# One phase of a two-block transformer kernel: the squares, sums and norm of the memory tokens in other slots of the output projection

## What is computed

```python
h = h + hybrid_mixer(rms_norm(h, norm_mix_g), ...)          # ends with concat([o, c]) @ w_out
h = h + memory_cross_attention(rms_norm(h, norm_xa_g),
                               rms_norm(mem, norm_mem_g), xa_wq, xa_wk, xa_wv, xa_wo)

# in the mixer, o comes from a gated delta rule with 8 heads of 128, c from a convolution:
o = rms_norm(o, dn_norm_g) * silu(z)       # the output norm, a mean of squares over each head
c = silu(layer_norm(c, cf_ln_g, cf_ln_b))
return concat([o, c], axis=-1) @ w_out     # phase "wout"

# rms_norm(x, g) = x * rsqrt(mean(x * x, axis=-1) + 1e-6) * g
k = mem_n @ w_k                            # phase "memk", the next one
```

## Time and profile before

| | us |
|---|---|
| median of 3 runs | 2903.57 |
| lowest, highest | 2901.63, 2904.53 |
| the profiled execution, its time | 2901.38 |
| its span, first to last instruction | 2899.6 |
| TensorE busy | 2817.0 |
| VectorE busy | 2066.1 |
| ScalarE busy | 1357.9 |

### The profile page before, as it was taken

One profiled execution on the slowest core, in us unless ns is written; L12 is line 12 of the kernel. 1 busy time (PEld: TensorE's weight loads), 2 busy tenths in 40 slices (PEclk: granted clock), 3 DMA queues, 4 the chain that ended last, 5 costly groups with the idle time before them and its releaser, 6 DMA issues.

```text
span 2899.6 us, 55174 instructions
## 1 busy us (share of the span) xinstructions
PE 2817.0 (97%) x23814; PEld 2768.6 (95%) x23814; DVE 2066.1 (71%) x2866; ACT 1357.9 (47%) x1723; POOL 4.6 (0%) x12
## 2 busy tenths in 40 slices
PE   7999998999999999999999999999989999999998
PEld 7999998999999999999999999997789999999998
DVE  7988755888869787787777866545566665675675
ACT  4445453444434553544545545455445544553453
POOL 0000000000000000000000000000000000000000
PEclk9999998999999999999999999999999999999999
DMA  6555204678747777777777765433245566556553
GB/s 237 182 175 165 68 8 155 209 275 288 261 152 250 288 279 279 285 282 283 293 275 273 277 219 189 163 122 124 89 149 199 194 198 191 194 188 201 191 188 124
DMA packets 160516, 591.59 MB, mean 204 GB/s; under 512 B 17840, under 2 KB 17840, under 8 KB 159760
## 3 DMA queue, kind: packets, MB, share of 16 engines
q1 hardware_dynamic: 159408, 580.45, 57.9%
q0 software_dynamic: 864, 7.60, 0.7%
HBM read 585.88 MB, written 2.10 MB: 203 GB/s over the span
## 4 chain that ended last, share of the span: by engine, by line
PE 88%; DVE 7%; ACT 2%; issue 1%; DMA 1%; SPq 0%; DVEq 0%; ACTq 0%
PE bank L485 79%; DVE wlo L1597 2%; PE bank L827 1%; DVE modacc L1583 1%; PE bank L690 1%; PE bank L505 1%; ACT whi L1015 1%; PE bank L704 1%; PE bank L522 1%; PE bank L526 1%; PE bank L795 1%; PE bank L805 1%; DVE tmp L1776 0%; PE bank L794 0%; PE bank L514 0%
## 5 line engine op out<-in xcount | busy, mean ns | idle before, releaser
L485 PE MATMUL bank<-act,whi 128*128 128x256 f32 x10144 | 1765.2, 280 | 44.3 <-DVE wlo L1597 28.7
L485 PEld LDWEIGHTS bank<-act,whi 128*128 128x128 f32 x10144 | 1546.3, 190 | 50.2 <-DVE wlo L1597 25.8
L1597 DVE TENSOR_TENSOR wlo<-raw,whi 128x1024 fp32r<-128x1024 f32 x906 | 1096.5, 1222 | 453.0 <-ACT whi L1015 450.9
L485 PE MATMUL bank<-act,wlo 128*128 128x256 f32 x5072 | 1413.9, 279 | 0.0
L1015 ACT ACTIVATE whi<-raw 128x1024 fp32r<-128x1024 f32 x906 | 943.3, 1057 | 779.2 <-PE bank L485 778.5
L485 PEld LDWEIGHTS bank<-act,wlo 128*128 128x128 f32 x5072 | 962.5, 190 | 0.0
L485 PE MATMUL bank<-hid,whi 128*128 128x256 f32 x3456 | 590.2, 277 | 1.5 <-DVE wlo L1597 1.5
L485 PEld LDWEIGHTS bank<-hid,whi 128*128 128x128 f32 x3456 | 520.8, 188 | 1.9 <-DVE wlo L1597 1.3
L485 PE MATMUL bank<-hid,wlo 128*128 128x256 f32 x1728 | 478.2, 277 | 0.0
L1583 DVE SCALAR_TENSOR_TENSOR modacc<-modraw,small,modacc 128x512 f32<-128x512 f32 x480 | 348.3, 746 | 18.9 <-DMA modraw<-mods 13.6
L485 PEld LDWEIGHTS bank<-hid,wlo 128*128 128x128 f32 x1728 | 324.9, 188 | 0.0
(11 more groups left out here) (363 smaller groups left out, 1519.5 us busy)
## 6 DMA issues: line engine op xcount, KB each, us to landing
raw<-stream SPq DMA_DIRECT2D x906, 512.0 KB, 4.6
modraw<-mods SPq DMA_DIRECT2D x192, 512.0 KB, 4.5
h<-x_t SPq DMA_DIRECT2D x4, 512.0 KB, 5.2
memV<-mem_t POOLq DMA_DIRECT2D x1, 2048.0 KB, 8.5
tmp<-ctx_t POOLq DMA_DIRECT2D x1, 2048.0 KB, 9.7
out_t<-tmp SPq DMA_DIRECT2D x4, 512.0 KB, 2.6
cz<-catt POOLq DMA_DIRECT2D x1, 1216.0 KB, 11.6
bias<-na_bias POOLq DMA_DIRECT2D x1, 1024.0 KB, 5.2
```

The costliest lines, as they stand in the source:

```text
L485: mm = pe.matmul(b[:, hf * T:(hf + 1) * T], lhs, rhs, start=(kc == 0 and hf == 0 and n == 0), stop=(kc == ph.chunks - 1 and n == 2), skip_ ...
L1597: ve.tensor_tensor(wlo[:, at % SPL_N, :], raw[:, at % RAW_N, :], whi[:, at % SPL_N, :].bitcast(F32), ALU.subtract).then_inc(split_done, 1)
```

## The change

Three things are moved or exchanged:

- ScalarE's four squares of memory go from (0, 4), all at once, to (1, 0) to (1, 3), one per slot, with the wait for the load at (1, 0).
- VectorE's four strided reductions at (0, 7) become, one quarter per slot at (1, 1) to (1, 4), two plain additions each: 128x512, then 128x256.
- The steps of the norm follow: row sums from (1, 3) to (1, 7), mean from (1, 6) to (2, 2), square root from (1, 7) to (2, 3), reciprocal from (2, 0) to (2, 4), spreading from (2, 2) to (2, 5).
- On TensorE, slot 1 comes ahead of the row sums of the output norm, directly behind slot 0.

```diff
             def memory_root(i, j):
-                if (i, j) == (1, 3):
+                if (i, j) == (1, 7):
                     pe.wait_ge(mem_sum, 1)
...
-                if (i, j) == (2, 2):
+                if (i, j) == (2, 5):
                     norm_root(3, ROOT, root)
...
-            c.at(act_ready, 1)
-            next(wout)
+            for n in range(2):
+                c.at(act_ready, n + 1)
+                next(wout)
             for hd in range(DN_H):
                 c.at(on_act, hd // 4 + 1)
                 for mt in range(TT):
                     mm = row_sums(bank[4][:, 2 * hd + mt:2 * hd + mt + 1], tmp[:, hd, :], slice(mt * P, (mt + 1) * P), True, True)
             mm.then_inc(on_pe, 1)
-            c.at(act_ready, 2)
-            next(wout)
             c.at(on_dve, 2)
...
             def memory_squares(i, j):
-                if (i, j) == (1, 7):
+                if (i, j) == (2, 3):
                     c.at(var, 1)
                     sc.activation(small[:, ROOT:ROOT + TT], small[:, ROOT:ROOT + TT], ACT.Sqrt).then_inc(std, 1)
                     c.end(var, 1)
-                if isinstance(i, int) and i == 0 and j == LAG + 1:
-                    sc.wait_ge(mem_in, 16)
-                    for q in range(4):
-                        sc.activation(tmp[:, 4 * q:4 * q + 4, :], memory[:, 4 * q:4 * q + 4, :], ACT.Square).then_inc(mem_sq, 1)
+                if i == 1 and j < 4:
+                    if j == 0:
+                        sc.wait_ge(mem_in, 16)
+                    sc.activation(tmp[:, 4 * j:4 * j + 4, :], memory[:, 4 * j:4 * j + 4, :], ACT.Square).then_inc(mem_sq, 1)
...
             def memory_sums(i, j):
-                if (i, j) == (1, 6):
+                if (i, j) == (2, 2):
                     c.at(sums, 1)
...
-                if (i, j) == (2, 0):
+                if (i, j) == (2, 4):
                     c.at(std, 1)
...
-                if isinstance(i, int) and i == 0 and j == PH["wout"].S - 1:
-                    for q in range(4):
-                        c.at(mem_sq, q + 1)
-                        ins = ve.tensor_reduce(memK[:, q, :],
-                                               tmp[:, 4 * q:4 * q + 4, :].rearrange("p k t -> p t k"), AX.X, ALU.add)
-                    ins.then_inc(mem_sum, 1)
+                if i == 1 and 1 <= j <= 4:
+                    q = j - 1
+                    c.at(mem_sq, q + 1)
+                    sq = tmp[:, 4 * q:4 * q + 4, :]
+                    chain(ve.tensor_tensor(sq[:, 0:2, :], sq[:, 0:2, :], sq[:, 2:4, :], ALU.add))
+                    ins = ve.tensor_tensor(memK[:, q, :], sq[:, 0, :], sq[:, 1, :], ALU.add)
+                    if q == 3:
+                        ins.then_inc(mem_sum, 1)
```

## The result

The changed kernel takes 2888.58 us (median of 4 runs, 2887.83 to 2889.97). The kernel before took 2904.05 us beside it (4 runs, 2901.63 to 2905.33). The ratio is 0.9945, with an interval of 0.9934 to 0.9957: faster by 12.5 to 19.2 us, the medians 15.5 apart. The forecast was 2890.8, in a range of 2887.5 to 2896.0. The profiled execution took 2889.14 us, its span is 2887.3; the profiled pair is thus 12.2 us apart in time and 12.3 in span. Among the experiments' executions, one of experiment 1 (4750.46 us) and one of the kernel before beside it (3165.69 us) had a granted clock of 0.56 and 0.84 where all others have 0.99; the medians count them, the ratios do not.

The account below looks back on a forecast made before the run. TensorE, busy 97% of the span, was taken as the bound, so only its stalls or lower clock pay. 12.8 + 0.4 - 0.4 = 12.8 us off 2901.38 gave 2888.6; 2.2 for the median made 2890.8, range 2887.5 to 2896.

Parts of the forecast that it names:

- (a): TensorE slots 5 to 7: waits of 7.67 and 2.34 us go, slot 8 starts at 467.6 instead of 480.41, 12.8 us won.
- (b): Second body: the moved squares and additions fit on ScalarE and VectorE beside TensorE's 22.6 us; cost taken as zero.
- (c): ScalarE's moved wait for memory, behind the split of slot 8: under a microsecond of waiting, counted as zero cost.
- late-memory rival: Memory lands beyond 465.5 us as raw loads take half of the bytes, costing 1 to 4 us; chance 0.08.
- (d): Memory's norm, moved later: VectorE's waits for row sums and spread cost TensorE zero, one microsecond if VectorE's idle time is gone.
- (e): Output norm at the phase's start, slot 1 ahead of the row sums: gain between -0.1 and 0.85 us, 0.4 taken.
- (f): TensorE's full-clock pace, 113.5 or 118 ns per multiplication: slots 8 to 11 may keep the slower one; -0.4 us taken.
- Slower: Rival: pace falls to 118 ns in long stretches behind the phase; 600 us of it gives 2914.8 us; chance 0.03.
- Does the gain stay: Behind the phase: the next phase's 3.5 us entry stall stays and comes earlier by the same time, gain expected whole.

Follow-up runs that it names:

- experiment 1: Changed kernel with TensorE's old order put back (slot 0, output norm's row sums, slot 1): 2890.29 us, ratio 0.9953 to the kernel before.
- experiment 9: The changed kernel itself run once more, nothing edited, beside three variants: 2889.02 us, ratio 0.9945 to the kernel before.
- Experiment 5: Changed kernel with the four squares and their wait for memory's load back at (0, 4) on ScalarE: 2901.33 us, ratio 0.9990 to the kernel before.
- experiment 4: Kernel before with eight additions replacing the four strided reductions at the old place (0, 7): 2902.53 us, ratio 0.9995 to the kernel before.
- experiment 3: Changed kernel with strided reductions, one per slot at the new places, instead of the two additions: 2892.55 us, ratio 0.9961 to the kernel before.
- experiment 6: Changed kernel with POOL's two transfers swapped, so memory comes behind the 1.2 MB one: 2891.46 us, ratio 0.9953 to the kernel before.
- experiment 2: Kernel before with only slot 1 put ahead of the output norm's row sums on TensorE: 2906.99 us, ratio 1.0007 to the kernel before.
- Experiment 8: Changed kernel with TensorE's spreading of memory's root one slot later, at (2, 6): 2890.23 us, ratio 0.9949 to the kernel before.

## Why the prediction was right, point by point

**(a) The two stalls: right.** 12.8 us were forecast for the start of slot 8; from slot 3 to slot 8, 12.73 came, and 13.24 in the second profile of the changed kernel (experiment 9). Slot 5 starts directly behind slot 4, at 457.57. Experiment 5 shows which edit does it (12.3 us of it back with the squares in the first body), experiment 4 how little the reductions were (2.1).

**(b) The second body has room: right.** The additions take 0.68 and 0.43 us as in the earlier trace rows; TensorE doesn't wait there. That even reductions of 2.05 us would have fitted (experiment 3) the sum didn't ask.

**(c) The moved wait: the size was off, the price wasn't.** "Under a microsecond" was 2.42. Two terms made it: ScalarE was done with the split of slot 8 at 459.0 and not 460.4, as TensorE ran about 1.6 us earlier from slot 3 on; and memory landed at 461.4 and not 460.8. It cost nothing, since a lead of 3.0 us was left behind it (experiment 6). The load lands so late because it is issued late, at 452.3 us before and 452.1 after, when TensorE is in slot 2 or 3: the memset that it waits for is ahead of the phase in VectorE's order only. Whether it could be issued earlier was not tried.

The late-memory rival is out, and its premise, weight loads that take half of the bytes, did not come. The queues (packets, MB, share) while memory was under way, first in the changed kernel with five weight loads beside it, then before with one, answer to the earlier trace rows:

```profile
q0 software_dynamic: 191, 2.55, 74.0%
q1 hardware_dynamic: 107, 0.44, 11.4%
...
raw<-stream SPq DMA_DIRECT2D x5, 512.0 KB, 10.4
memV<-mem_t POOLq DMA_DIRECT2D x1, 2048.0 KB, 9.3
```

```profile
q0 software_dynamic: 172, 2.37, 72.1%
q1 hardware_dynamic: 87, 0.36, 10.2%
```

Five loads moved hardly more than one. Memory needed 9.3 us here and 8.5 before, but 9.2 to 9.5 in experiments 2, 4 and 5 too, which have one load beside it, and 8.9 to 9.8 in the others with POOL's transfers in this order. So the 0.8 us is not the loads' doing; the 8.5 us is the lowest of the thirteen. The rival's sum took 2.85 MB for what POOL's queue moved up to the landing, where the trace has 2.37: with that, its own halving lands memory near 463.6, short of both 464.3 and 465.5.

The Trainium skill (DMA: Bandwidth & Descriptors, Queues, rings and completion order) has each engine take turns between the rows it has work for, a whole packet at a time. By that and the packet sizes of these lines (13.4 KB against 4.1), an estimate, memory's queue would keep some 77%, if the packets of the profile are those of the page. This trace has 85% up to the landing, and 74% over 452.1 to 465 us (3.34 of 4.50 MB, the landed memory and then the 1.2 MB behind it), so the rule is not borne out here by its numbers; that it gave the landing at 461.6, with 2.85 MB in the sum, was luck.

**(d) Memory's norm: right.** VectorE waits 2.13 us for the sums (2.02 before) and 0.79 for the spread, TensorE for neither. Experiment 8 shows that 3.50 would be free as well. The changed kernel's VectorE timeline:

```profile
490.78 0.16 DVE L1997 TENSOR_SCALAR small<-bank 128x2 f32<-128x2 f32 x1 [2.13 <-PE bank L522]
```

**(e) The output norm: right in size, by terms at the edges of what was given.** TensorE's timeline, and the stretch in which the spreading starts, answer to the earlier trace rows:

```profile
436.78 3.63 PE L522 MATMUL bank<-ones,tmp 128*128 128x1 f32 x32
...
441.20 5.47 PE L526 MATMUL bank<-ident,small 128*128 128x128 f32 x32 [0.80 <-DVE small L1980]
449.04 0.50 PE L485 MATMUL bank<-act,whi 128*128 128x256 f32 x2 [2.37 <-DVE act L1989]
...
441.00:444.00 3.00, 2.80 (x13) 2.80 (x14) 0.90 (x2) 0.00 (x0) 0.00 (x0) 0.55 0.00 0
```

The spreading starts 9.96 us behind slot 0 instead of 10.82, 0.86 us won where 0.85 was said. It falls to half clock, as feared, and takes 5.47 us instead of 3.73, so that slot 2 comes 0.4 us later behind slot 0 than before. In return slot 2 runs at full clock, 2.84 us instead of 4.24. Net, 1.0 us by slot 3 where 0.4 were taken, inside the stated -1.5 to 2.2. All of it is the order's own (experiment 1 takes 21.65 us to slot 3, as before), and without the memory part it is nothing in the total (experiment 2). Its two parts, the earlier spreading and the clock in slot 2, were both named; the 0.4 was the middle of a range and no sum.

**(f) Pace: the mechanism right, the size too small.** 0.4 us were charged (the three figures given there add up to 0.3), and from slot 8 to the next phase the changed kernel lost 1.5 (70.35 us against 68.86). It holds 118 ns over the last ten slots of the phase, where before has 113.5. The same kernel profiled again (experiment 9) doesn't. Both for 516 to 524 us, L485 alone, with the columns of the earlier trace rows:

```profile
516.00:524.00 8.00, 8.00 (x70) 8.00 (x69) 1.00 0.72 260
```

```profile
516.00:524.00 8.00, 8.00 (x73) 8.00 (x72) 1.00 0.76 268
```

Experiment 9's phase is 103.0 us long, the first profile's 105.2, both of one kernel. So this term is not fixed by the kernel, and should have been a spread of some 2 us and not -0.4. Whether the change makes the slower pace more frequent is open: the last eight slots of the phase take 22.6 us in five of the fourteen profiles, all of kernels with both parts of the change (nine profiles), and 21.8 us in the other four of these and in all five without. The rival "Slower" asked for 600 us at the slower pace; behind slot 4 of the next phase the ledger moves by 0.6 us in all, over 2300 us.

**Does the gain stay: yes, within about a microsecond.** The entry stall of the next phase went from 3.5 to 3.1 us (3.5 in experiment 9):

```profile
PE bank L485 <- DVE wlo L1596: 3.1, 1, 3.1
```

From there the gain stays at 12.3 us up to the context load, loses 0.8 there, comes back by 1.3 near 2150 us, where nothing was edited, and is 12.8 at the last slot.

**The total.** For the profiled execution 2888.6 us were forecast and 2889.14 came. The mechanism carries this, but the closeness is in part luck. In the ledger the forecast's 12.8 + 0.4 - 0.4 came as 12.73 + 1.02 - 1.48, and 0.60 us won ahead of the phase, for which the sum had no term, made up for what the pace took.

The median of the forecast lay 2.2 us above that for the profiled execution, because the profiled execution of before lay 2.2 below its median. The changed kernel's median lies 0.6 below its profiled execution. The miss of the forecast is 2.2 us, and the weak step is that last addition: a single execution's distance to its median was carried over as if it belonged to the kernel. It belongs to the execution. The 12.3 us of the profiled pair and the 15.5 of the medians differ by 3.2; the second profile of the changed kernel (span 2885.1) is 14.5 below before's, and before's median was 2904.6 to 2905.2 beside the experiments. That covers the difference in size, but which stretches of before make its usual execution longer than its profiled one can't be read from one profile, and stays open.

## What to carry to other kernels

A wait for a transfer costs what is queued behind it on its engine, so it belongs behind the work that is ready by then, and the work that it releases is to be spread over the following slots: here that is 12 us, the cheaper additions only two at the old place and nothing at the new one, and the reordering on TensorE nothing while that wait stood behind it and 1 us once it was gone. Measure how far a moved wait is from biting by making it later on purpose (memory by 4 us, the spread by 2.7) instead of trusting a sum. And put a forecast of a median on a median of several runs, with the profile used for the differences alone.

## What the runs showed of the hardware that was not expected

The pace of back-to-back multiplications at full clock has two values, 113.5 and 118 ns (73 or 70 records in 8 us), and which one holds over ten slots changes between executions of one kernel: 1.1 us. What sets it stayed open.

Sixteen float32 multiplications with one moving column (32 records), without a gap in 3.63 us, are followed by a stretch at a granted clock of 0.55 (0.63 before), so most of it at the lower level of 1.2 GHz. That holds in both orders: slot 1 came next before, the spreading after.

A 512 KB weight load beside the 2 MB load of memory takes about twice its usual time: 10.1 us (median of six, 452.1 to 465 us) against a median of 4.5 over the whole execution, and 9.5 to 10.6 us as the only one beside it (before, experiments 2, 4 and 5). The 2 MB load takes 8.5 to 9.5 us beside one such load and 8.9 to 9.8 beside several, so the number of small loads hardly matters to it. Beside the context load the small ones take 11.1 to 12.3 us, and a small tile that is needed soon is the one that suffers, 500 us away from the edit under study: the same 16 slots there took from 51.0 to 55.8 us in kernels that don't differ in them.
